# Sparse layer of a hybrid decoder: one old-key block turned earlier, one normalisation later, selection rounds dealt anew

## The reference, cut to what matters

```python
def indexer_select(iq, iw, ik, q_pos, k_pos, topk):
    s = jnp.einsum('bqhd,bsd->bqhs', iq, ik) * (IDX_DIM ** -0.5)
    score = jnp.einsum('bqh,bqhs->bqs', iw * (IDX_HEADS ** -0.5), jax.nn.relu(s))
    score = jnp.where(causal[None], score, -jnp.inf)
    _, idx = lax.top_k(score, topk)
...
def sparse_attend(q, k_sel, v_sel, valid):
    s = jnp.einsum('bqhd,bqkhd->bqhk', q, k_sel) * (DSA_HEAD_DIM ** -0.5)
    p = jax.nn.softmax(jnp.where(valid[:, :, None, :], s, -jnp.inf), axis=-1)
    return jnp.einsum('bqhk,bqkhd->bqhd', p, v_sel)
```

## Time and profile before

| | |
|---|---|
| median of three runs | 1134.51 us |
| the profiled execution | 1133.51 us |
| its span, first to last instruction | 1131.8 us |
| TensorE busy | 1096.7 us, 97% |
| VectorE, ScalarE, GpSimd busy | 671.4, 489.8, 388.1 us |
| mean granted clock of TensorE | 0.998 of 2.4 GHz |
| index scores of layer 1 | from 278.9 us |
| first half of the keys | from 285.0 us |
| first page pair | at 386.9 us |
| last page pair | at 549.8 us |

### The profile page before, as it was taken

How to read it: one execution, slowest core, us unless ns; L and a number is a source line. 1 busy time by engine, 2 the same in 40 slices (tenths; PEclk the granted TensorE clock), 3 DMA queues, 4 the chain that set the end, 5 groups by cost and what they waited for, 6 DMA issues and landing times. The chain is left out here.

```text
span 1131.8 us, 25807 instructions
## 1 busy us (share of the span) xinstructions
PE 1096.7 (97%) x10675; PEld 956.1 (84%) x10675; DVE 671.4 (59%) x1235; ACT 489.8 (43%) x959; POOL 388.1 (34%) x327
## 2 busy tenths in 40 slices
PE   8999999899999999999999999999999999999897
PEld 6889887899758987889955599999999889988796
DVE  6462355755999679777454645596455272255642
ACT  6542377642434222222364554332444352367643
POOL 5545132343313423114300045354334245312330
PEclk9999999999999999999999999999999999999999
DMA  5335235142315776883779962232230334344202
GB/s 171 108 113 167 94 112 188 61 124 70 118 41 187 242 256 215 271 290 114 261 300 409 373 205 77 74 112 84 95 113 3 112 106 149 103 131 131 85 28 79
DMA packets 126698, 168.97 MB, mean 149 GB/s; under 512 B 19288, under 2 KB 92288, under 8 KB 126575
## 3 DMA queue, kind: packets, MB, share of 16 engines
q1 hardware_dynamic: 114569, 152.75, 40.5%
q10 hardware_dynamic: 12014, 14.59, 3.9%
HBM read 150.86 MB, written 16.81 MB: 148 GB/s over the span
## 5 line engine op out<-in xcount | busy, mean ns | idle before, releaser
L758 POOL TENSOR_TENSOR w_lo<-raw,w_hi 128x512 fp32r<-128x512 f32 x265 | 357.1, 1380 | 639.5 <-ACT w_hi L1542 639.4
L794 PE MATMUL psum<-h_hi,w_hi 128*128 128x272 f32 x1584 | 462.0, 292 | 7.2 <-DVE h_lo L2476 5.5
L796 PE MATMUL psum<-h_hi,w_lo 128*128 128x272 f32 x1584 | 457.7, 289 | 0.0
L795 PE MATMUL psum<-h_lo,w_hi 128*128 128x272 f32 x1584 | 455.8, 288 | 0.0
L794 PEld LDWEIGHTS psum<-h_hi,w_hi 128*128 128x128 f32 x1584 | 297.3, 188 | 20.7 <-issue 18.7
L795 PEld LDWEIGHTS psum<-h_lo,w_hi 128*128 128x128 f32 x1584 | 297.6, 188 | 0.1
L796 PEld LDWEIGHTS psum<-h_hi,w_lo 128*128 128x128 f32 x1584 | 296.9, 187 | 0.0
L1542 ACT ACTIVATE w_hi<-raw 128x1024 fp32r<-128x1024 f32 (+1 forms) x135 | 133.3, 1033 | 111.8 <-PE psum L796 77.1
L794 PE MATMUL psum<-w_hi,h_hi 128*128 128x512 f32 (+2 forms) x352 | 124.6, 354 | 0.9 <-issue 0.8
L795 PE MATMUL psum<-w_lo,h_hi 128*128 128x512 f32 (+2 forms) x352 | 121.2, 344 | 0.0
L796 PE MATMUL psum<-w_hi,h_lo 128*128 128x512 f32 (+2 forms) x352 | 121.1, 344 | 0.0
(11 more groups left out here) (332 smaller groups left out, 1368.1 us busy)
## 6 DMA issues: line engine op xcount, KB each, us to landing
smp_keys<-in_cache_k_dram SPq DMA_DIRECT2D x128, 256.0 KB, 4.4
raw<-in_gla_w_in_dram SPq DMA_DIRECT2D x23, 1024.0 KB, 5.9
raw<-in_dsa_w_in_dram SPq DMA_DIRECT2D x17, 1024.0 KB, 5.5
spare<-in_cache_v_dram SPq DMA_DIRECT2D x34, 512.0 KB, 8.1
raw<-in_cache_v_dram SPq DMA_DIRECT2D x30, 512.0 KB, 8.3
gla_s_in<-in_state_gla_dram SPq DMA_DIRECT2D x16, 512.0 KB, 7.3
raw<-in_gla_w_out_dram SPq DMA_DIRECT2D x8, 1024.0 KB, 6.4
out_dram<-gla_s_in ACTq DMA_DIRECT2D x16, 512.0 KB, 3.6
```

The costliest lines, as they stand in the source:

```text
L758: pool.tensor_tensor(pair_view(w_lo, key)[:, k], raw_view(key)[:, k], pair_view(w_hi, key)[:, k].bitcast(F32), ALU.subtract)\
L794: pe.matmul(out, lh, rh, start=start, stop=False)
L795: pe.matmul(out, lh, rl, start=False, stop=False)
L796: return pe.matmul(out, ll, rh, start=False, stop=stop)
```

## The change

It has three parts, all in layer 1.

First, the old index keys. `turn_old(0)` is issued within the key projection, ahead of the decode tile of its second weight item, where it was issued after that projection and after the wait for `iq_seq`. On ScalarE its copy stands between the evictions of tile 3 and of the decode tile. The projection's five tiles no longer take their banks from the common rotation but from `(3, 6, 7, 0, 1, 2)`, so that banks 4 and 5 are left out, and the common counter is raised five times less.

Second, the 32 rounds of the decode selection: `eights` goes from (17, 1, 1, 1, 3, 2, 2, 2) to (17, 1, 4, 2, 2, 1, 1, 1). Both add up to 29.

Third, `sample_norm(0)` is run after page pair 12 is turned, where it was run after pair 11.

```diff
@@ tensor, dsa @@
-                t_job([(L, "k", 0, kh) for kh in range(2)], (L, "k", 0), BLK, "k_st", range(NBANK))
-
-                pe.wait_ge(*on("iq_seq", L))
-
                 def turn_old(b):
...
-                turn_old(0)
+                def first_old(x, t):
+
+                    if (x, t) == (1, SMP):
+                        turn_old(0)
+
+                t_job([(L, "k", 0, kh) for kh in range(2)], (L, "k", 0), BLK, "k_st", (3, 6, 7, 0, 1, 2), first_old)
+                pe.wait_ge(*on("iq_seq", L))
                 for b in range(DB):
@@ scalar, dsa @@
+                def old_key(b):
+                    act.wait_ge(*on("idx_turned", L, b))
+                    if b >= 2:
+                        act.wait_ge(*on("idx_s", L, "old", b - 2))
+                    copy(ik_old[:, b % 2, :], psum[:, bank_of("oldT", L, b), :]).then_inc(*sig("ik_old", L, b))
+
                 def k_rows(n):
                     for t in range(TILES):
+                        if n == 0 and t == SMP:
+                            old_key(0)
...
                 k_rows(0)
-                for b in range(DB):
-                    act.wait_ge(*on("idx_turned", L, b))
-                    if b >= 2:
-                        act.wait_ge(*on("idx_s", L, "old", b - 2))
-                    copy(ik_old[:, b % 2, :], psum[:, bank_of("oldT", L, b), :]).then_inc(*sig("ik_old", L, b))
+                for b in range(1, DB):
+                    old_key(b)
                     if b == 1:
                         after_item(L, "k", 0, 1)
@@ vector, dsa @@
-                eights = (17, 1, 1, 1, 3, 2, 2, 2)
+                eights = (17, 1, 4, 2, 2, 1, 1, 1)
...
                     if p == 10:
                         top(bias_p[2][:], P, 2)
+                    if p == 12:
+                        sample_norm(0)
                     if p == 11:
-                        sample_norm(0)
                         top(bias_p[2][:], P, 2)
                         masked(2)
```

## The result

The changed kernel takes 1139.97 us (median of 11 runs, 1136.71 to 1143.04), the kernel before 1134.09 us in as many (1131.58 to 1135.09): a ratio of 1.005 with an interval of 1.0039 to 1.0061, or 5.7 us slower (4.4 to 6.9). The forecast was 1138.0.

A forecast was written before the change was run, and what follows sets the result against it. TensorE, busy 1096.7 of 1131.8 us, was taken to bound the kernel. The terms +4.45 - 0.1 + 0.75 + 0 - 1.6 made +3.5 us, so 1138.0 us against the median of 1134.51; range 1133.3 to 1141.0.

The forecast's parts named there:

- The sum: Whole kernel: all terms added, without a fall of the clock, +3.5 us, 1138.0 us against the median; chance 0.46.
- the rival of the clock: Key projection: TensorE's clock falls in the new gap of over 4 us, costing 1.3 us more, 1139.3 us; chance 0.28.
- The first key half's banks: Key projection, first tile: waits for bank 6's reader, the relu of the fourth tile's head 1; +4.45 us.
- Old keys ahead: Old index keys: ScalarE's chain has no slack, so gaps move ahead of the second and third groups; -0.1 us.
- The counter five behind: Key projection, second half: gets banks 1 to 5 and waits for VectorE's copies of the decode scores; +0.75 us.
- Rounds: Selection rounds dealt anew over the page pairs: they fit in VectorE's waits for pages; 0 us.
- Normalisation: Page pair 12: with the normalisation one pair later, TensorE's gap there goes; -1.6 us.
- the short wait: First key half: rotation begins at bank 3, waits 1.65 us in place of 4.45, 1135.2 us, not slower; chance 0.15.
- The closed gaps without a bank wait: Old keys and page pair 12: aimed gaps of 1.57 and 1.61 us close, no bank wait opens, 1131.0 us; chance 0.05.
- The late pair: Page pair 3: one round past the page's landing stalls 1.2 us, perhaps once more, 1139 to 1141 us; chance 0.06.

The follow-up runs named there:

- Experiment 1: Changed kernel with its first key half in banks 7, 1, 2, 3, 6, nothing else; 1132.7 us, ratio 0.9991 to the kernel before.
- experiment 5: Changed kernel with 18 unused matmuls into bank 1 filling the wait ahead of the first key half; 1137.85 us, ratio 1.0034 to the kernel before.
- experiment 8: Kernel of experiment 2 with the early turn of the first old keys undone on TensorE and ScalarE; 1132.51 us, ratio 0.9993 to the kernel before.
- experiment 2: Kernel of Experiment 1 with the common bank counter raised by five behind the first key half; 1132.17 us, ratio 0.9984 to the kernel before.
- Experiment 3: Kernel of experiment 2 with ScalarE's weight split moved behind all the old keys; 1130.85 us, ratio 0.9987 to the kernel before.
- experiment 7: Changed kernel, its tuple kept, with the common bank counter raised by five behind the first key half; 1137.84 us, ratio 1.004 to the kernel before.
- experiment 10: Kernel of experiment 2 with the normalisation back behind page pair 11; 1133.31 us, ratio 0.9994 to the kernel before.
- experiment 4: Kernel before with only the normalisation moved behind page pair 12; 1132.16 us, ratio 0.9987 to the kernel before.
- experiment 6: Changed kernel with the banks of the first key half in the order 3, 6, 7, 0, 1; 1134.08 us, ratio 1.0001 to the kernel before.
- experiment 9: Kernel of experiment 2 with the old deal of selection rounds (17, 1, 1, 1, 3, 2, 2, 2); 1132.03 us, ratio 0.9982 to the kernel before.

## Why the prediction was right, point by point

The forecast was a change for the worse of 3.5 us, or 4.8 with the clock's fall; the runs have 5.7 (4.4 to 6.9). The sum alone lies below that interval and the rival of the clock inside it. So what happened is the prediction's second case, to which it gave 0.28, and not its first, with 0.46: the bank wait and its size were right, and the clock term that the sum left out was 1.5 us. The steps, in their order:

- **The first key half's banks: +4.45 forecast, +4.43 found**, released by the relu that was named. Experiment 1 takes it away with the tuple alone.
- **The clock in the new gap** was left out of the sum and given as the likeliest rival, at 1.3 us. It happened: this is where the sum fell short. A stretch of 3.41 us at half the clock costs half of it in lost work, 1.7 us if all of it is matmuls; the ledger has 1.5, and experiment 5, which keeps the lateness but not the idleness, is 1.54 us shorter in that stretch. The argument against it, that the fall in the trace of before came where little work was left, fell: here the work went on right behind the gap, and the clock was down all the same. That is what the Trainium skill (TensorE: Matmul & The Clock Gate, section "HAM oscillation — how this bites in real kernels") says of an engine left idle between bursts; the traces agree, with 4.59 us idle and then a clock of 0.50.
- **Old keys ahead: -0.1 forecast, -0.34 found** (0.39 between experiments 8 and 2). The mechanism was right: ScalarE's chain holds, and the gaps move to the second and third groups. Experiment 3 shows it for the third group, by taking the split out of that chain. The gaps sum to 1.39 us in place of 1.57; that accounts for 0.2, and the rest of the step is not explained.
- **The counter five behind: +0.75 forecast, +0.78 found**, released by the copies of the scores; experiments 7 and 2 have no such wait.
- **Rounds: 0 forecast, 0 found.** The bias is ready at 471.94 + 0.70, 2.6 us ahead of the matmuls that want it at 475.26.
- **Normalisation: -1.6 forecast, -1.68 found at pair 12**; 0.46 us come back at pair 15. The prediction named pair 13, by its page, as late next; it was pair 15, and by its page too. VectorE had ended the normalisation at 514.12, and it stands for the DMA ahead of pair 15's second piece in after (first row) as in before (second):

```profile
555.47 2.31 DVE L2594 STREAM_TRANSPOSE smp_keys<-smp_keys 128x2048 f32<-128x2048 f32 x1 [0.79 <-DMA smp_keys<-in_cache_k_dram]
...
547.08 2.31 DVE L2587 STREAM_TRANSPOSE smp_keys<-smp_keys 128x2048 f32<-128x2048 f32 x1 [0.36 <-DMA smp_keys<-in_cache_k_dram]
```

  VectorE starts on that piece 10.2 us behind the end of pair 14's matmuls in after, 9.5 in before and 9.0 to 10.3 in the twelve traces, and TensorE stands wherever it is over 9.9. The gap has 0.2 to 0.5 us in six of the ten traces with the later normalisation, and is absent in before and experiment 10; whether the normalisation's place has a part in it isn't shown. Experiments 4 and 10 have 1.5 and 1.1 us for the net, with intervals that hold both 1.2 and 1.7.

With these sizes the sum is 4.43 + 1.5 - 0.34 + 0.78 - 1.2 = 5.2 us, or 4.7 without pair 15; both lie inside the measured interval.

Of the rivals, the short wait is excluded for the changed kernel by the 4.59 us, though experiment 6 shows that its arithmetic was sound. The closed gaps without a bank wait are experiment 2, 1.8 us faster where 3.2 us of gaps were there to be had: 1.39 us of it only move to the next copies. The late pair did not occur at pair 3; a small one did at pair 15.

Two parts of the change thus make the kernel faster, the early turn by its traces alone (0.3 to 0.4 us); the deal of the rounds shows no effect, and the bank bookkeeping that came with the first part costs 6.7 us by the ledger (4.43 + 1.5 + 0.78), against the 1.5 to 2.0 that they gain. Experiment 2 mends it with one tuple and one line, and is 1.8 us faster than before. Experiment 3 has the lowest median, 1130.85 us, and by its trace saves another 0.9 us, but its ratio is no lower than that of experiment 2, so these runs don't show it to be the faster one.

## What to carry to other kernels

A PSUM bank rotation is part of the schedule: whoever moves a job to a rotation of its own must look up, bank by bank, which read comes last before its first tile, and what the common rotation now hands to the jobs behind. An in-order engine waits for the bank it is dealt even where others are free; one tuple of bank numbers was worth 5.9 us here by the ledger, and 6.7 by experiment 1. And a gap of an engine that is the bound costs more than its length where the clock falls behind it, so price both. A wait can also move without changing the total, as at the old keys here: add up the gaps of the whole stretch before counting one as a loss or a gain.

## What the runs showed of the hardware that was not expected

- **The clock falls behind shorter gaps too, but not each time.** Ahead of 212 us, in layer 0, lies a gap of 1.73 to 1.77 us, the longest of the earlier trace rows; in experiments 4 and 8 the clock fell 0.9 and 0.7 us after TensorE had gone on behind it, in before, after and the other experiments not. In experiments 6 and 10 it fell in layer 3, at 1069.0 and 1070.4 us, behind a gap of 1.75 us, and in experiment 5 at 498.5, behind a stop of 1.6 us. Each of these falls shows 3.4 us at 0.50, as that of the changed kernel behind its 4.59 us gap; the fall inside the 4.58 us gap of experiment 7 lasted 6.83 us.
- **What a fall costs depends on the work behind it.** It was 1.5 us at the key projection and behind page pair 1, where matmul follows matmul, and 2.2 us for the long fall of experiment 7. In layer 0 it was 1.0 us (from the gap to the first index score 67.75 us in experiment 4, 66.74 in before), in layer 3 0.9 (from the gap to the end of the span 63.4 us in experiments 6 and 10, 62.5 in before). Which it will be in a given execution these runs do not say.
- **TensorE stops with no releaser.** In page pair 1, ahead of the 123rd matmul, it stood 0.69 us in the trace of before, 2.40 in that of after, 1.79 in experiment 1, 0.42 in 2, 1.24 in 4, 0.69 in 6, 2.34 in 8 and 0.97 in 10, and not at that place in 3, 5, 7 and 9. Behind two of these (after and experiment 8) the clock fell as well, so that the place costs between nothing and some 4 us. That is as much as these kernels' runs differ among themselves, and it is why this document puts no weight on the spans of single traces. It is not the only such place: ahead of the 119th matmul of page pair 5 TensorE stood 1.13 us in before, 0.89 in after and 0.33 to 1.43 in six experiments, and experiments 5 and 9 have stops of 1.4 to 1.6 us elsewhere. In the packets of the traces a 16 KB transfer of the instruction queue starts 2.2 to 2.5 us before TensorE goes on, in all 19 of these stops (404.93 and 407.32 in after, 397.38 and 399.61 in before). Where the 123rd matmul of pair 1 did not wait, the latest such transfer had started 2.2 to 5.0 us before it. That TensorE waits for its own instructions there fits all twelve traces, but it is argued; no run tested it.
